# First loads reordered, warm-up without a load, and one weight split moved ahead of the first gates

## The chip, the cores and the metric

The kernel runs on one core of one Trainium2 chip. The metric is the device time of one execution in microseconds (us). Three runs of the kernel before gave 2299.57, 2301.09 and 2301.11, the median being 2301.09.

## The reference

A first block and a second block, each of two layers, work on `x` of 256 tokens by 1024 channels in float32. Each layer has a feed-forward part, a mixer and a second feed-forward part. The change touches only the start of the first feed-forward part of all:

```python
h = rmsnorm(x, g_ffn1[l])                       # x * rsqrt(mean(x^2) + 1e-6) * g
x = x + 0.5 * ((silu(h @ w1) * (h @ w3)) @ w2)  # w1, w3: 1024 x 2816, w2: 2816 x 1024
```

The mixers (Fourier, short convolution and pooling in the first block; window attention and gated linear attention in the second) follow, and the result is 256 x 1024 float32.

## The kernel before

All weights, some 400 MB, are streamed once, so every matmul works on a weight that has just arrived. A weight unit is 128 partitions by 2048 float32 columns, 1 MB, loaded by the SP engine into one of three `raw` buffers (`RAW = 3`) as two DMAs of 512 KB with 4 KB per partition. To keep float32 accuracy each weight and each activation is split in two rounded halves: ScalarE copies `raw` into `whi` (`split` at L1129), VectorE subtracts to get `wlo` (`split` at L1581), and TensorE multiplies hi by hi, hi by lo and lo by hi. `whi` and `wlo` have four slots (`HL = 4`). The semaphores are `raw_in` (loaded), `hi_done` (ScalarE's half), `w_ready` (VectorE's half, which also lets SP load the raw buffer anew), and `w_used` (multiplied, which lets ScalarE write the slot anew). SP's load of unit u waits until unit u - 3 is split on VectorE; SP issues its loads strictly in order, each waiting in front of all that follow.

In a feed-forward part unit b (0 to 21) holds, for one block of 128 hidden channels, the columns of the gate and of the up matrix for all eight 128-row chunks of the 1024 inputs. `hidden_chunks` (L640 to L660) multiplies it: 32 matmuls in 16 pairs, one of 512 columns (L656) and one of 256 (L657), into one of three pairs of PSUM banks. ScalarE's `low_parts(b)` copies the low part out (L1196), VectorE's `summed` adds it (L1710) and frees the banks (`pair_free`), `gate_scaled` multiplies the gate by `rstd_row` (L1715), ScalarE's `gates` applies Silu (L1202), VectorE's `hidden` multiplies by the up part (L1720), and ScalarE's `hidden_hi` (L1207) and VectorE's `hidden_lo` (L1726) split the result. These steps and the splits stand in one hand-written order on each engine.

The norm is spread over the part: the matmuls take x times the gain only; 1/rms comes in by `rstd_row`. It needs `x` in the token layout: ScalarE squares it (L1160) after both 512 KB loads of `x` have landed (`x_in`, 32), takes the root, VectorE refines it and makes a diagonal matrix with the identity (`rstd_diag`, L1660 to L1665), and TensorE spreads it (`rstd_spread`, L706) between the second and third chunk of unit 3. ScalarE copies the result to `rstd_row` (L1231), and only then can the gates of units 0 and 1 be done; the gates of unit 2 and the splits of units 5 and later follow these.

For the very first part the activations come transposed from the host (`t_xt`), in four pieces of two chunks, 256 KB with 2 KB per partition. They are multiplied by the norm weight columns `vecs` on ScalarE (L1154) and split on VectorE (L1612). The first halves of units 0 and 1 come as pieces of their own too (`first_piece`, L428). The identity and `vecs` (128 x 144) are loaded from ScalarE's queue. TensorE waits for the identity and runs `WARM = 16` transposes whose result nobody uses (L1105), then `begin` (L665 to L682): unit 0 chunks 0 and 1, unit 0 chunks 2 and 3, unit 1 chunks 0 to 3, then the upper halves of units 0 and 1, each when its split and its activations are there.

Of the kernel before, what the change touches and what calls it, by code (L numbers as in the profile page):

```python
# [27 lines left out]
P = 128  # L28
# [5 lines left out]
FG = FF // 256  # L34
FC = FF // P
EPS = 1e-6
WARM = 16
PAIR = (0, 2, 1)
SPACER = 40
RAW = 3  # L40
# [23 lines left out]
V_FOLDED = V_FINAL + DC  # L64
V_GAIN = {"ffn0": 0, "mix": DC, "ffn1": 2 * DC}
V_CONV = V_OUT_NORM = 3 * DC
FIRST_PARTS = tuple(slice(2 * i, 2 * i + 2) for i in range(4))


HEADS, KV_HEADS, HEAD_DIM = 8, 2, 64  # L70
# [78 lines left out]
def rows_of(first, n):  # L149
    return slice(first, first + n)  # L150
# [21 lines left out]
def build(nc, a, known):  # L172
# [4 lines left out]
    def semaphore(name):  # L177
        return ctx.enter_context(nc.semaphore(name))
# [7 lines left out]
    with ctx:  # L186
# [153 lines left out]
        x_in = semaphore("x_in")  # L340
        ident_in = semaphore("ident_in")
        vecs_in = semaphore("vecs_in")
        xt_part_in = [semaphore(f"xt_part_in{i}") for i in range(4)]
        warm = semaphore("warm")
        first_m = semaphore("first_m")
        out_ready = semaphore("out_ready")
# [57 lines left out]
        def _(eng):  # L404
# [21 lines left out]
            def first_piece(u, first, cols, signal):  # L426

                eng.dma_start(raw[:, u, first:first + cols], a["t_gate_up_1a"][rows_of(u * P, P), first:first + cols]  # L428
                              ).then_inc(signal, 16)
# [87 lines left out]
            def xt_part(i):  # L517
                cols = FIRST_PARTS[i]
                eng.dma_start(xt_in[:, cols, :], a["t_xt"].rearrange("p (c t) -> p c t", c=DC)[:, cols, :]
                              ).then_inc(xt_part_in[i], 16)  # L520
# [3 lines left out]
            xt_part(1)  # L524
            first_piece(0, 512, 512, first_in[1])
            first_piece(1, 0, 1024, first_in[2])
            for u in range(2):
                xt_part(2 + u)
                for j in range(2):
                    first_piece(u, 1024 + 512 * j, 512, raw_in[u])  # L530
            for u in (2, 3):
                gate_up(a["t_gate_up_1a"], u, u)
            for m in range(MT):
                eng.dma_start(x[:, m, :], a["x"][0, m * P:(m + 1) * P, :]).then_inc(x_in, 16)
            for _ in e.layers(1):
                ffn_loads(0, a["t_gate_up_1a"], a["w2_a"])
                if e.layer() == 0:
                    eng.dma_start(cs[:, :, :], a["t_cs"].rearrange("(m p) n -> p m n", p=P)).then_inc(tables1_in, 16)
                    eng.dma_start(cc[:, :], a["t_cc"]).then_inc(tables1_in, 16)
                    eng.dma_start(poolm[:, :, :, :], a["t_pool"].rearrange("(m p) (g t) -> p m g t", p=P, g=4)  # L540
                                  ).then_inc(tables1_in, 16)
                mix1_loads(FFN_UNITS)
                ffn_loads(FFN_UNITS + MIX_UNITS[1], a["t_gate_up_1b"], a["w2_b"])
# [25 lines left out]
        def _(eng):  # L569
# [530 lines left out]
                assert u + 2 == u0 + MIX_UNITS[2]  # L1100

            eng.sem_inc(w_used, HL)
            eng.wait_ge(ident_in, 16)
            for _ in range(WARM):
                nc.tensor.transpose(psum[:, 5, 0:P], ident[:, :], ident[:, :])  # L1105
            for _ in e.layers(1):
                ffn_tensor(0, 0, "mix")
                mix1_tensor(FFN_UNITS)
# [8 lines left out]
        def _(eng):  # L1117
# [71 lines left out]
            def ffn_scalar(u0, f, next_stage):  # L1189
                stage = f"ffn{f}"  # L1190

                def low_parts(b):

                    multiplied(u0 + b)
                    first = 2 * PAIR[b % 3]
                    nc.scalar.activation(low[:, b % 2, :, :], psum[:, first:first + 2, T:2 * T], ACT.Copy).then_inc(  # L1196
                        low_done, 1)

                def gates(b):

                    eng.wait_ge(scaled_done, ffn_blocks(e, f, b))
                    nc.scalar.activation(gate[:, b % 2, :], gate[:, b % 2, :], ACT.Silu).then_inc(gate_done, 1)  # L1202

                def hidden_hi(b):

                    eng.wait_ge(hid_done, ffn_blocks(e, f, b))
                    nc.scalar.activation(ht_hi[:, b, :], hid[:, b % 2, :], ACT.Copy).then_inc(ht_hi_done, 1)  # L1207

                if stage == "ffn0" and (e.block, e.lay) == (2, 0):
                    eng.wait_ge(x_whole, wholes(e))  # L1210
                    final_squares(1, 0).then_inc(acted, e.mark(acted, ("ss", "final")))
                    eng.wait_ge(xgf_done, 2)
                    final_squares(1, 1).then_inc(acted, e.mark(acted, ("ss", "ffn0")))
                    x_hi(stage, 1)
                elif e.unit(u0) > 0:
                    x_hi(stage, 1)
                else:
                    split(2)
                    low_parts(0)
                    split(3)  # L1220
                    low_parts(1)
                    eng.wait_ge(x_in, 32)
                stage_start(stage, u0, [junk[:, m, :] for m in range(MT)])
                if e.unit(u0) > 0:
                    low_parts(0)
                    split(u0 + 4)
                    low_parts(1)
                else:
                    split(u0 + 4)
                eng.wait_ge(small, e.after(small, ("rstd", stage)))  # L1230
                nc.scalar.activation(rstd_row[:, :], psum[:, 6, 0:T], ACT.Copy).then_inc(  # L1231
                    acted, e.mark(acted, ("rstd", stage)))
                for b in range(2):
                    gates(b)
                split(u0 + 5)
                for b in range(2):
                    hidden_hi(b)
                for b in range(2, FC):
                    low_parts(b)
                    gates(b)  # L1240
                    hidden_hi(b)
                    split(u0 + b + 4)
                for s in range(2 * FG + 1, FFN_UNITS):
                    if s == 2 * FG + 6:
                        if next_stage == "ffn0":
                            eng.wait_ge(folded, 1)
                        if next_stage != "end":
                            x_hi(next_stage, 0)
                        if next_stage == "ffn0" and (e.block, e.lay) == (1, LAYERS - 1):
                            final_squares(0, 0)  # L1250
                            eng.wait_ge(xgf_done, 1)
                            final_squares(0, 1)
                    split(u0 + s + 3)
# [281 lines left out]
                split(u0 + 37)  # L1535
                split(u0 + 38)

            eng.dma_start(ident[:, :], a["t_ident"]).then_inc(ident_in, 16)
            eng.dma_start(vecs[:, 0:V_FOLDED], a["t_vecs"]).then_inc(vecs_in, 16)
            eng.wait_ge(warm, 1)  # L1540
            nc.scalar.activation(ms[:, :], rt[:, :], ACT.Copy)
            eng.wait_ge(vecs_in, 16)
            eng.wait_ge(xt_part_in[0], 16)
            first_hi_of(0, 0)
            eng.wait_ge(w_used, 2)
# [6 lines left out]
            eng.wait_ge(first_in[2], 16)  # L1552
            nc.scalar.activation(whi[:, 1, 0:1024], raw[:, 1, 0:1024], ACT.Copy).then_inc(first_hi, 1)
            for u in range(2):
                eng.wait_ge(xt_part_in[2 + u], 16)
                first_hi_of(1, u)
                split(u)
            for _ in e.layers(1):
# [11 lines left out]
        def _(eng):  # L1570
# [133 lines left out]
            def ffn_vector(u0, f, next_stage):  # L1704
# [30 lines left out]
                if e.unit(u0) == 0:  # L1735
                    split(u0 + 2)
                    first_summed(0)
                    split(u0 + 3)
                    first_summed(1)
                    norm(stage, rstd)  # L1740
                    rstd_diag(stage)
                else:
                    stage_start(stage, u0, 1)
                if e.unit(u0) == 0:
                    fold = vecs[:, V_FOLDED:V_FOLDED + DC]
                    nc.vector.tensor_tensor(fold, vecs[:, V_FINAL:V_FINAL + DC], vecs[:, V_BASE[2]:V_BASE[2] + DC],
                                            ALU.mult).then_inc(folded, 1)
# [7 lines left out]
                eng.wait_ge(acted, e.after(acted, ("rstd", stage)))  # L1755
                for b in range(2):
                    gate_scaled(b)
                for b in range(2):
                    hidden(b)
                for b in range(2):  # L1760
                    hidden_lo(b)
                for b in range(2, FC):
                    eng.wait_ge(low_done, ffn_blocks(e, f, b))
                    e.link(summed(gate, b, 0))
                    gate_scaled(b)
                    summed(up, b, 1).then_inc(pair_free, 1)
                    eng.wait_ge(pair_free, ffn_blocks(e, f, b))
                    hidden(b)
                    split(u0 + b + 3)
                    hidden_lo(b)  # L1770
                split(u0 + FC + 3)
                for s in range(2 * FG + 1, FFN_UNITS - 1):
# [414 lines left out]
                split(u0 + 37)  # L2187

            nc.vector.memset(rt[:, :], 1.0).then_inc(warm, 1)
            eng.sem_inc(w_ready, RAW)  # L2190
            eng.sem_inc(x_whole, 1)
            eng.wait_ge(ident_in, 16)
            eng.wait_ge(vecs_in, 16)
            eng.wait_ge(xt_part_in[0], 16)
            first_lo_of(0, 0)
            for k in range(2):
# [9 lines left out]
            nc.vector.tensor_tensor(wlo[:, 1, 0:1024], raw[:, 1, 0:1024], whi[:, 1, 0:1024], ALU.subtract).then_inc(  # L2206
                first_ready, 1)
            for u in range(2):
                eng.wait_ge(xt_part_in[2 + u], 16)
                first_lo_of(1, u)  # L2210
                split(u)
            for _ in e.layers(1):
# [80 lines left out]
```

## Time and profile before

| what | us |
|---|---|
| median of three runs | 2301.09 |
| profiled execution, its own time | 2298.62 |
| its span, first to last instruction | 2296.8 |
| TensorE busy | 2277.3 |
| VectorE busy | 1537.3 |
| ScalarE busy | 1242.2 |

The page lists TensorE (PE) with 11,756 matmuls at 99% of the span. DVE is VectorE, ACT is ScalarE, SP the engine that issues most DMAs, PEld the weight loads of TensorE. A time in a row of the timeline is the start, in us from the first instruction, followed by the duration; what stands in brackets is the idle time of that engine just before, and what ended it. The mean granted clock of TensorE over the span is 0.998 of full speed.

### The profile page before, as it was taken

To read this page: it belongs to the slowest core of one execution; us is meant where nothing else is said; L and a number is where in the kernel's file an instruction comes from. 1 tells how busy PE (TensorE), PEld (TensorE's weight loads), DVE (VectorE), ACT (ScalarE), POOL (GpSimd) and SP (SyncE) were. 2 spreads that over 40 slices of the span, in tenths; PEclk is the share of its full clock that TensorE was granted. 3 is DMA by queue.
4 is the path that set the end of the run, shared out by engine and by line. 5 is a ranking of instruction groups with operands and counts; after the bars stand their busy time and mean duration, and the time that the engine had idled before them with its cause. 6 is when DMAs were issued, how large, how long until landed. Compare 5 with 4: busy or idle time off the path is not lost.

```text
span 2296.8 us, 29070 instructions
## 1 busy us (share of the span) xinstructions
PE 2277.3 (99%) x11756; PEld 1932.9 (84%) x11756; DVE 1537.3 (67%) x2156; ACT 1242.2 (54%) x1484; POOL 0.2 (0%) x4
## 2 busy tenths in 40 slices
PE   8999999999999999999999999999999999999999
PEld 7887888888888788888888888788888888878887
DVE  6764566765774466775776587667657747866773
ACT  6544445554653544654654585455456547645652
POOL 0000000000000000000000000000000000000000
PEclk9999999999999999999999999999999999999999
DMA  7556455555555445555555543545545545345553
GB/s 253 200 196 217 152 178 184 188 206 174 184 192 193 160 166 196 183 196 185 194 187 194 195 161 106 193 160 195 200 175 188 202 163 184 107 150 187 198 183 129
DMA packets 175802, 416.52 MB, mean 181 GB/s; under 512 B 16658, under 2 KB 21394, under 8 KB 175668
## 3 DMA queue, kind: packets, MB, share of 16 engines
q1 hardware_dynamic: 175380, 414.52, 52.2%
q8 instruction: 93, 1.52, 0.3%
q14 instruction: 41, 0.34, 0.0%
q10 hardware_dynamic: 288, 0.14, 0.0%
HBM read 413.55 MB, written 1.05 MB: 181 GB/s over the span
## 4 chain that ended last, share of the span: by engine, by line
PE 95%; DVE 2%; DMA 1%; ACT 1%; issue 0%; SPq 0%; ACTq 0%; DVEq 0%
PE psum L656 27%; PE psum L592 16%; PE psum L594 16%; PE psum L593 16%; PE psum L657 14%; PE psum L624 2%; DVE split_w L1581 1%; PE psum L928 1%; PE psum L756 1%; DMA raw<-t_gate_up_1a_dram 0%; PE psum L906 0%; PE psum L773 0%; DMA x<-x_dram 0%; ACT split_w L1129 0%; PE psum L897 0%
## 5 line engine op out<-in xcount | busy, mean ns | idle before, releaser
L1581 DVE TENSOR_TENSOR split_w<-raw,split_w 128x2048 fp32r<-128x2048 f32 (+2 forms) x408 | 886.2, 2178 | 308.4 <-ACT split_w L1129 307.3
L656 PE MATMUL psum<-xt,split_w 128*128 128x512 f32 x2816 | 982.7, 394 | 2.2 <-DVE split_w L1581 1.7
L1129 ACT ACTIVATE split_w<-raw 128x2048 fp32r<-128x2048 f32 (+2 forms) x408 | 740.8, 1824 | 331.5 <-PE psum L594 295.4
L657 PE MATMUL psum<-xt,split_w 128*128 128x256 f32 x2816 | 785.1, 279 | 0.0
L656 PEld LDWEIGHTS psum<-xt,split_w 128*128 128x128 f32 x2816 | 527.8, 187 | 124.5 <-DVE split_w L1581 2.1
L657 PEld LDWEIGHTS psum<-xt,split_w 128*128 128x128 f32 x2816 | 530.9, 189 | 0.3
L592 PE MATMUL psum<-split_w,xt 128*128 128x512 f32 (+1 forms) x736 | 292.8, 398 | 6.3 <-DVE split_w L1581 6.3
L594 PE MATMUL psum<-split_w,xt 128*128 128x512 f32 (+1 forms) x736 | 284.8, 387 | 0.0
L593 PE MATMUL psum<-split_w,xt 128*128 128x512 f32 (+1 forms) x736 | 284.8, 387 | 0.0
L592 PE MATMUL psum<-split_w,ht_hi 128*128 128x512 f32 x700 | 273.0, 390 | 0.0
L594 PE MATMUL psum<-split_w,ht_lo 128*128 128x512 f32 x700 | 272.5, 389 | 0.0
L593 PE MATMUL psum<-split_w,ht_hi 128*128 128x512 f32 x700 | 272.4, 389 | 0.0
L1710 DVE TENSOR_TENSOR gate<-psum,low 128x256 f32<-128x256 f32 x176 | 74.6, 424 | 155.4 <-ACT low L1196 155.2
L592 PEld LDWEIGHTS psum<-split_w,xt 128*128 128x128 f32 x736 | 139.0, 189 | 37.9 <-DVE split_w L1581 6.2
L594 PEld LDWEIGHTS psum<-split_w,xt 128*128 128x128 f32 x736 | 138.9, 189 | 28.5
L593 PEld LDWEIGHTS psum<-split_w,xt 128*128 128x128 f32 x736 | 139.2, 189 | 26.6 <-issue 1.0
L1196 ACT ACTIVATE low<-psum 128x512 f32<-128x512 f32 x176 | 104.6, 594 | 103.0 <-PE psum L657 102.7
L1202 ACT ACTIVATE gate<-gate 128x256 f32<-128x256 f32 x176 | 73.0, 418 | 161.3 <-DVE gate L1715 161.3
L594 PEld LDWEIGHTS psum<-split_w,ht_lo 128*128 128x128 f32 x700 | 131.4, 188 | 27.5
L592 PEld LDWEIGHTS psum<-split_w,ht_hi 128*128 128x128 f32 x700 | 131.4, 188 | 27.1
L593 PEld LDWEIGHTS psum<-split_w,ht_hi 128*128 128x128 f32 x700 | 131.4, 188 | 26.8
L1207 ACT ACTIVATE ht_hi<-hid 128x256 fp32r<-128x256 f32 x176 | 72.5, 416 | 90.4 <-DVE hid L1720 90.4
(272 smaller groups left out, 1730.8 us busy)
## 6 DMA issues: line engine op xcount, KB each, us to landing
raw<-w_in_dram SPq DMA_DIRECT2D x180, 512.0 KB, 4.4
raw<-t_gate_up_1b_dram SPq DMA_DIRECT2D x88, 512.0 KB, 4.1
raw<-t_gate_up_2a_dram SPq DMA_DIRECT2D x88, 512.0 KB, 4.1
raw<-t_gate_up_2b_dram SPq DMA_DIRECT2D x88, 512.0 KB, 4.1
raw<-t_gate_up_1a_dram SPq DMA_DIRECT2D x85, 512.0 KB, 4.1
raw<-ffn_w_down_dram SPq DMA_DIRECT2D x80, 512.0 KB, 4.3
raw<-w_a_dram SPq DMA_DIRECT2D x40, 512.0 KB, 4.1
raw<-w_b_dram SPq DMA_DIRECT2D x40, 512.0 KB, 4.2
```

Source lines behind the costliest of these rows:

```text
L592: nc.tensor.matmul(pair(p, m)[:, out], hi[:, c, t], whi[:, slot, w], start=first, stop=False)
L593: nc.tensor.matmul(pair(p, m)[:, out], hi[:, c, t], wlo[:, slot, w], start=False, stop=False)
L594: last = nc.tensor.matmul(pair(p, m)[:, out], lo[:, c, t], whi[:, slot, w], start=False, stop=final)
L624: last = nc.tensor.transpose(bank[0:src.shape[1], i * T + m * P:i * T + (m + 1) * P], src, ident[:, :])
L656: nc.tensor.matmul(bank, whi[:, slot, w], xt[:, c, :, :], start=c == 0, stop=False)
L657: last = nc.tensor.matmul(bank[:, 0:T], wlo[:, slot, w], xt_hi[:, c, :], start=False, stop=c == DC - 1)
L1129: nc.scalar.activation(whi[:, u % HL, first:n], raw[:, r, first:n], ACT.Copy).then_inc(hi_done, 1)
L1196: nc.scalar.activation(low[:, b % 2, :, :], psum[:, first:first + 2, T:2 * T], ACT.Copy).then_inc(low_done, 1)
L1202: nc.scalar.activation(gate[:, b % 2, :], gate[:, b % 2, :], ACT.Silu).then_inc(gate_done, 1)
L1207: nc.scalar.activation(ht_hi[:, b, :], hid[:, b % 2, :], ACT.Copy).then_inc(ht_hi_done, 1)
L1581: nc.vector.tensor_tensor(wlo[:, u % HL, first:n], raw[:, r, first:n], whi[:, u % HL, first:n], ALU.subtract).then_inc(w_ready, 1)
L1710: return nc.vector.tensor_tensor(out[:, b % 2, :], bank[:, 0:T], low[:, b % 2, j, :], ALU.add)
```

## The change

The edits, in the order of the diff:

- The activations come in three pieces: chunks 0-1, 2-3, and 4-7 (512 KB, 4 KB per partition). The last one is issued ahead of the upper halves of units 0 and 1, which come as two DMAs of 64 partitions with 4 KB per partition in place of two of 128 partitions with 2 KB.
- ScalarE's queue issues only the eight columns of `vecs` that the first norm needs, under a semaphore of its own (`gains_in`). The identity goes to SP's queue, behind unit 3 and ahead of `x`; the remaining 136 columns of `vecs` follow behind `x`.
- TensorE's warm-up is 11 float32 matmuls of 128 columns on zeros that VectorE writes to `junk`, in place of 16 transposes of the identity. It waits for that memset.
- VectorE waits for the identity at `rstd_diag` and for `vecs` at the fold behind it; ScalarE waits for `vecs` ahead of the first gates.
- In the first feed-forward part ScalarE does `low_parts(2)` and the split of unit 5 ahead of the first two gates, where the split stood behind them; VectorE does its split of unit 5 behind the two products with `rstd_row` and ahead of `hidden(0)`, where it stood behind `hidden(2)`. All other parts keep their order.

```diff
-WARM = 16
+WARM = 11
-FIRST_PARTS = tuple(slice(2 * i, 2 * i + 2) for i in range(4))
+FIRST_PARTS = (slice(0, 2), slice(2, 4), slice(4, 8))
...
             first_piece(1, 0, 1024, first_in[2])
+            xt_part(2)
             for u in range(2):
-                xt_part(2 + u)
-                for j in range(2):
-                    first_piece(u, 1024 + 512 * j, 512, raw_in[u])
+                for j in range(2):
+                    part = slice(64 * j, 64 * j + 64)
+                    eng.dma_start(raw[part, u, 1024:2048], a["t_gate_up_1a"][rows_of(u * P + 64 * j, 64), 1024:2048]
+                                  ).then_inc(raw_in[u], 16)
             for u in (2, 3):
                 gate_up(a["t_gate_up_1a"], u, u)
+            eng.dma_start(ident[:, :], a["t_ident"]).then_inc(ident_in, 16)
             for m in range(MT):
                 eng.dma_start(x[:, m, :], a["x"][0, m * P:(m + 1) * P, :]).then_inc(x_in, 16)
+            eng.dma_start(vecs[:, DC:V_FOLDED], a["t_vecs"][:, DC:V_FOLDED]).then_inc(vecs_in, 16)
...
-            eng.wait_ge(ident_in, 16)
+            eng.wait_ge(warm, 2)
             for _ in range(WARM):
-                nc.tensor.transpose(psum[:, 5, 0:P], ident[:, :], ident[:, :])
+                nc.tensor.matmul(psum[:, 5, 0:P], junk[:, 0, 0:P], junk[:, 0, 0:P], start=True, stop=True)
...
+                if e.unit(u0) == 0:
+                    eng.wait_ge(pair_free, ffn_blocks(e, f, 0))
+                    low_parts(2)
+                    split(u0 + 5)
+                    eng.wait_ge(vecs_in, 16)
                 for b in range(2):
                     gates(b)
-                split(u0 + 5)
+                if e.unit(u0) > 0:
+                    split(u0 + 5)
                 for b in range(2):
                     hidden_hi(b)
                 for b in range(2, FC):
-                    low_parts(b)
+                    if e.unit(u0) > 0 or b > 2:
+                        low_parts(b)
...
-            eng.dma_start(ident[:, :], a["t_ident"]).then_inc(ident_in, 16)
-            eng.dma_start(vecs[:, 0:V_FOLDED], a["t_vecs"]).then_inc(vecs_in, 16)
+            eng.dma_start(vecs[:, 0:DC], a["t_vecs"][:, 0:DC]).then_inc(gains_in, 16)
             eng.wait_ge(warm, 1)
             nc.scalar.activation(ms[:, :], rt[:, :], ACT.Copy)
-            eng.wait_ge(vecs_in, 16)
+            eng.wait_ge(gains_in, 16)
...
                     norm(stage, rstd)
+                    eng.wait_ge(ident_in, 16)
                     rstd_diag(stage)
                 else:
                     stage_start(stage, u0, 1)
                 if e.unit(u0) == 0:
+                    eng.wait_ge(vecs_in, 16)
                     fold = vecs[:, V_FOLDED:V_FOLDED + DC]
...
                 for b in range(2):
                     gate_scaled(b)
+                if e.unit(u0) == 0:
+                    split(u0 + 5)
...
-                    split(u0 + b + 3)
+                    if e.unit(u0) > 0 or b > 2:
+                        split(u0 + b + 3)
...
             nc.vector.memset(rt[:, :], 1.0).then_inc(warm, 1)
+            nc.vector.memset(junk[:, 0, 0:P], 0.0).then_inc(warm, 1)
...
-            eng.wait_ge(ident_in, 16)
-            eng.wait_ge(vecs_in, 16)
+            eng.wait_ge(gains_in, 16)
```

## Rows read from the trace of the kernel before

**Rows 1.** The page: the span, and busy time of each engine.

```profile
span 2296.8 us, 29070 instructions
PE 2277.3 (99%) x11756; PEld 1932.9 (84%) x11756; DVE 1537.3 (67%) x2156; ACT 1242.2 (54%) x1484; POOL 0.2 (0%) x4
```

**Rows 2.** Waits of PE, whole span: us in total, times, longest.

```profile
PE psum L592 <- DVE split_w L1581: 9.3, 6, 2.7
...
PE psum L656 <- DVE split_w L1581: 1.7, 2, 1.2
```

**Rows 3.** Timeline of the head: start us, us, engine, line.

```profile
0.73 0.41 ACTq L1538 DMA_DIRECT2D ident<-t_ident_dram  x1
...
4.05 3.67 PE L1105 MATMUL psum<-ident 128*128 128x128 f32 x16 [4.05 <-DMA ident<-t_ident_dram]
...
5.47 0.91 ACT L1154 ACTIVATE xt<-xt_in,vecs 128x256 fp32r<-128x256 f32 x2 [2.32 <-DMA vecs<-t_vecs_dram]
...
8.05 0.80 PE L656 MATMUL psum<-xt,split_w 128*128 128x512 f32 x1 [0.32 <-DVE split_w L2199]
```

**Rows 4.** DMA issues at 0.73, 1.16 and 4.54: KB, us to landing.

```profile
xt_in<-t_xt_dram SPq DMA_DIRECT2D x1, 256.0 KB, 3.1
vecs<-t_vecs_dram ACTq DMA_DIRECT2D x1, 72.0 KB, 4.3
...
raw<-t_gate_up_1a_dram SPq DMA_DIRECT2D x1, 256.0 KB, 7.7
```

**Rows 5.** Instructions on the tile `ones`: min/median/max ns.

```profile
L1661 DVE MEMSET ones<- x1: 165/165/165, 27.6 to 27.6; 128x128 f32 x1
```

**Rows 6.** Timeline of PE at 1380 us, float32 matmuls.

```profile
1380.25 1.05 PE L928 MATMUL psum<-sm 128*128 128x128 f32 x8
```

**Rows 7.** One-us stretches: busy by engine, then PE clock, DMA share, GB/s.

```profile
7.00:8.00 1.00, 0.72 (x4) 0.32 (x2) 1.00 (x3) 1.00 (x3) 0.00 (x0) 1.00 0.97 244
...
12.00:13.00 1.00, 1.00 (x7) 0.87 (x7) 0.83 (x2) 0.72 (x1) 0.00 (x0) 1.00 1.02 395
```

**Rows 8.** Chain that ended last, 12 to 23 us: start us, us.

```profile
13.37 1.24 DVE split_w L1581
14.62 0.33 SPq L415
...
15.95 6.86 DMA x<-x_dram
```

**Rows 9.** Timeline, 28 to 46 us.

```profile
28.24 0.70 PE L706 MATMUL psum<-diag,ones 128*128 128x256 f32 x2
...
29.76 1.28 ACT L1202 ACT_TABLE_LOAD   x1
31.71 0.75 DVE L1715 TENSOR_TENSOR gate<-gate,rstd_row 128x256 f32<-128x256 f32 x2
32.17 0.75 ACT L1202 ACTIVATE gate<-gate 128x256 f32<-128x256 f32 x2 [1.12 <-DVE gate L1715]
...
32.83 1.90 ACT L1129 ACTIVATE split_w<-raw 128x2048 fp32r<-128x2048 f32 x1
35.06 0.76 DVE L1726 TENSOR_TENSOR ht_lo<-hid,ht_hi 128x256 fp32r<-128x256 f32 x2 [1.68 <-ACT ht_hi L1207]
35.24 0.58 ACT L1196 ACTIVATE low<-psum 128x512 f32<-128x512 f32 x1
...
37.64 2.28 DVE L1581 TENSOR_TENSOR split_w<-raw,split_w 128x2048 fp32r<-128x2048 f32 x1
...
40.06 0.47 PE L656 MATMUL psum<-xt,split_w 128*128 128x512 f32 x1 [1.24 <-DVE split_w L1581]
...
42.27 2.28 DVE L1581 TENSOR_TENSOR split_w<-raw,split_w 128x2048 fp32r<-128x2048 f32 x1
...
45.69 0.39 PE L656 MATMUL psum<-xt,split_w 128*128 128x512 f32 x1
```

**Rows 10.** A slice of two us late in the span, columns as in rows 7.

```profile
1460.00:1462.00 2.00, 2.00 (x7) 1.57 (x6) 1.50 (x1) 0.00 (x0) 0.00 (x0) 0.54 0.76 260
```

More of the change, by code:

```diff
@@ L342, in build @@
         vecs_in = semaphore("vecs_in")
-        xt_part_in = [semaphore(f"xt_part_in{i}") for i in range(4)]
+        gains_in = semaphore("gains_in")
+        xt_part_in = [semaphore(f"xt_part_in{i}") for i in range(3)]
         warm = semaphore("warm")
@@ L1554, in _ @@
             for u in range(2):
-                eng.wait_ge(xt_part_in[2 + u], 16)
+                eng.wait_ge(xt_part_in[2], 16)
                 first_hi_of(1, u)
@@ L2208, in _ @@
             for u in range(2):
-                eng.wait_ge(xt_part_in[2 + u], 16)
+                eng.wait_ge(xt_part_in[2], 16)
                 first_lo_of(1, u)
```

## Prediction

> **What bounds the kernel now.** I read the page first: TensorE is busy for 99% of the span, so the kernel is a queue of matmuls and only an interval in which TensorE stands still, or runs slowly, can be won [rows 1]. The span is 2296.8 us and the profiled execution took 2298.62 us, that is 1.8 us around the span; the median of the runs shown is 2301.09, so 2.5 us above it. I make the sum as a difference on the profiled execution and set it against the median.
>
> The second view is what TensorE waited for. Matmuls of the mixers wait 9.3 us for VectorE, six times; a look at stretches of the span puts these behind 1250 us, in code that the change doesn't touch. In the first stage there are two waits for the split of weights (L1581), 1.7 us together [rows 2]. The timeline of the head shows the rest. TensorE does nothing until 4.05, when the identity has landed and the warm-up transposes can run; its first real matmul starts at 8.05. ScalarE starts on the activations at 5.47, released by the norm weights (`vecs`), and 2.58 us pass from there to 8.05 (two activation halves, a 512-column split on ScalarE, the same on VectorE) [rows 3]. The first real matmul pairs are slow (the first matmul took 0.80 us where later ones of the same shape take about 0.40).
>
> **Part 1, the first loads.** The norm weights are issued second on ScalarE's queue and land 4.3 us after their issue; the first activation piece, issued at 0.73 like the identity, lands after 3.1 us, so at 3.8 [rows 3, 4]. In the new kernel eight columns go first on that queue. I bound their landing from both sides by the 3.1 us and the 4.3 us of these two rows: 3.8 to 5.0, and take 3.8, the nearer in size. A weight piece of 256 KB follows and then lands near 5.0 (it was issued 0.45 us behind the activations and 136 KB of small rows are gone), which ScalarE reaches just then. So the first real matmul can start at 3.8 + 2.58 = 6.4, at most 7.6: 0.5 to 1.65 us earlier.
>
> A rule of the Trainium skill speaks against the eight columns: "DMA: Bandwidth & Descriptors", Specifications, says that transfers under 512 B are not at line rate because the engine reads, modifies and writes. The rows here are 32 B. It gives no time for so few of them; no row of this trace has 32 B either, and the bound of 5.0 us above doesn't use it.
>
> **The warm-up.** It no longer waits for the identity but for two memsets on VectorE; one of 128x128 takes 0.17 us [rows 5] and starts near 0.9, so TensorE starts at about 1.1. A float32 matmul is recorded as two passes; eight passes of 128x128 take 1.05 us at the full clock with the drain of the last [rows 6], 0.11 us each. The 16 transposes took 3.67 us in the cold state, 0.23 each [rows 3]. Eleven matmuls are 22 passes, 22 x 0.23 = 5.1 us, so they end at 6.2, just ahead of 6.4. If the passes did not overlap with their weight loads (0.42 each), the warm-up would end at 1.1 + 9.2 = 10.3. TensorE would then be busy for more than 5 us before the first real pair, where it was busy for 3.7 before: the slow first pairs, some 0.6 us over two pairs, should mostly be gone.
>
> **What follows in the head.** Each later piece is limited by its landing. Without the 136 KB, at about 290 GB/s at the head, all pieces come some 0.45 us earlier, those of the second stage too; then the upper activations come as one 512 KB piece ahead of the upper half of unit 0, where 256 KB stood before, which costs 256 KB at the 393 GB/s to be had there = 0.65 us. The upper half of unit 0 landed at 4.54 + 7.7 = 12.25 [rows 4, 7]. Rows of 4 KB instead of 2 KB work for it: the stretch with 2 KB and smaller rows moved 244 GB/s, the one at 12 us 395 [rows 7]; for the 768 KB changed that is between nothing and 768 KB x (1/0.244 - 1/0.395) = 1.2 us. I take 0.25, near the lower end, because 2 KB rows were also in flight at 395. The upper half of unit 0 lands at 12.25 - 0.45 + 0.65 - 0.25 = 12.2, between 11.3 and 12.5.
>
> This landing matters more than the first one. VectorE's split of unit 0 (ended at 14.6) frees the raw buffer for unit 3, whose load SP issues at 14.62, and behind it in the same queue stands `x`, which landed at 15.95 + 6.86 = 22.83 [rows 8]. Everything in the norm hangs on that landing. The identity now stands ahead of `x`: 64 KB, 0.17 us at 393 GB/s, 0.25 with its small rows. The shift of `x`'s landing is d = -0.05 + 0.2 = about +0.1, and by the bounds -0.7 to +0.5. The rest of `vecs` stands behind `x` and is asked for only at ScalarE's first gate and VectorE's fold, several us later. Unit 4's load, behind it, is 0.2 us later and had landed before 26, two us before its split.
>
> **Part 2, the sixth unit.** TensorE stopped at 38.82 and went on at 40.06, for VectorE's split of unit 5 (37.64, 2.28 us) [rows 9]. Now ScalarE, at 29.76 (where it loaded its table), first does `low_parts(2)` (0.58, pitch 0.50), then the split (1.90), to 32.16; the table load (1.28) and the two gates (0.75) follow to 34.1. VectorE has ended its two products with `rstd_row` at 31.71 + 0.75 = 32.46, then splits unit 5 to 34.7. So TensorE finds unit 5 ready 5 us early, and the 1.24 us go.
>
> What is late next: VectorE's `hidden(0)` comes behind that split, at 34.66; ScalarE's rounding at 35.07; VectorE's `ht_lo` at 35.5 where it was at 35.06. From here everything is 0.43 us later: `gates(2)`, `hidden(2)`, ScalarE's split of unit 6, then `low_parts(3)`, which was behind ScalarE's split of unit 6 before as well, and behind all that VectorE's split of unit 6, which was 42.27 to 44.55 [rows 9]. It now ends at 44.98 + d. TensorE began unit 6 at 45.69 (after unit 5 from 40.06), and would without a wait begin it at 45.69 - 1.24 = 44.45. So a wait of 0.6 us takes the place of the one of 1.24. Unit 7 follows 4.63 us behind unit 6 on VectorE (42.27 - 37.64) against 5.63 us of matmuls (45.69 - 40.06), so no later wait comes.
>
> Is the earlier head worth more? No: TensorE, if it comes to unit 3 earlier, waits at the spread of `rstd` (28.24 before, [rows 9]), which hangs on `x` by d. All that is won before it ends there. The sum: new start of unit 6 = 45.05 + d = 45.15, against 45.69: 0.55 us less. With 0.1 for small things I forecast 0.6 us less: 2298.0 on the profiled execution, 2300.5 on the median.
>
> The table load is where a rule and the trace differ. Before, the load at 29.76 stood behind a finished copy and cost 1.28 [rows 9]. The Trainium skill, "ScalarE: Activation LUTs", What ACT_TABLE_LOAD costs, adds a drain of about 1.38 us to each switch; by that the gates would end at 35.5 and the chain to unit 6 would be some 0.8 us later. The trace has nothing of that drain, and I go by 1.28.
>
> **The rivals.** (a) *The loads are faster than I count.* If 4 KB rows and the missing small rows bring `x` forward by 0.7 us (d = -0.7), unit 6 is ready at 44.35, the spread and all of TensorE's work behind it move too, and unit 6 begins at 44.35: 1.3 us less; with the bound of 1.2 us for the rows in full 1.9 less. That is 2299.8 to 2299.2. For it: 244 against 395 GB/s. Against it: that low rate belongs to the very first rows too, when queues fill.
>
> (b) *The upper activations in one piece delay everything.* The place is the landing of the upper half of unit 0, ahead of which 256 KB more now stand; the price goes one to one through the raw buffer of unit 3 to `x`, the norm and unit 6, with the identity's 0.25 on top. It decides from d = +0.64 (45.69 - 45.05). With nothing for rows and with columns of 32 B and 64-partition pieces each held up by some tenths, d is 0.5 to 1.2: slower by up to 0.6, 2301.5.
>
> (c) *The warm-up fails its purpose*: it ends at 10.3, or zeros leave the clock low. Then TensorE's first 32 pairs (5.63 / 16 = 0.352 us each, 11.3 us) end at 21.6, unit 2 at 27.2, and the spread, four pairs on, comes at 28.6, 0.4 late; without a wait unit 6 would start at 44.45 + 0.4 = 44.85, before it is ready. It is hidden, and the time is mine, 2300.5; clock staying low for 5 us longer would cost up to 2.5 us, 2302.
>
> (d) *The change doesn't do what it says*: TensorE still waits at unit 5 or an engine waits long for `vecs` or the identity: no change, 2301.1.
>
> **How the numbers follow.** My case 0.5, (a) 0.2, (b) 0.17, (c) with a loss and (d) 0.13 together. The measured medians also move: late in the span TensorE's granted clock fell to 0.54 in a slice of 2 us [rows 10], that is to its lower level of 1.2 GHz for most of it, after it had stood waiting for VectorE. That slice alone lost 2 x 0.46 = 0.9 us, it went on into the next, and it happened twice in this execution; I estimate 1.5 us for each, and suppose that their number differs between executions: the profiled one and the median differ by 2.5 us. So the range is 2297.8 to 2302.0. What a measurement can tell from no change is about 0.2%, 4.6 us; every case above lies inside it. Only something unseen gets out: 0.03 faster, 0.04 slower, 0.93 the same.
>
> **What would show it.** In the new profile: first warm-up matmul near 1.1, first real one at 6.2 to 7.6, the first pairs at 0.35 us; `x` landed at 22.1 to 23.3; no wait at unit 5 and a wait of 0.3 to 0.8 at unit 6; a small wait at the spread. I am wrong if TensorE reaches unit 7 more than 1.5 us earlier or any later than before, or if a wait for `vecs` shows up on ScalarE or VectorE.

## Result, and the profile after

The changed kernel took 2303.15 us (median of 20 runs, 2300.76 to 2305.33); the kernel before, run beside it, 2299.36 (20 runs, 2295.70 to 2301.93). The ratio is 1.0017, with a 95% interval of 1.0011 to 1.0024: 3.8 us slower, less than 0.2%, but clear of the noise. The forecast of 2300.5 us and its direction were wrong, and the time lies outside the range. The forecast started from 2301.09, the median of three runs; twenty runs put the kernel before at 2299.36, so as a difference the miss is larger: 0.6 us less was forecast, 3.8 us more was measured.

The page after, which answers to [rows 1]:

```profile
span 2302.6 us, 29085 instructions
PE 2279.3 (99%) x11762; PEld 1936.9 (84%) x11762; DVE 1537.9 (67%) x2157; ACT 1242.1 (54%) x1484; POOL 0.2 (0%) x4
```

The waits of TensorE over the span after (us in total, times, longest), for [rows 2]:

```profile
PE psum L597 <- DVE split_w L1592: 9.6, 6, 2.9
PE psum L661 <- DVE split_w L2215: 3.0, 2, 2.2
PE psum L661 <- DVE split_w L1592: 2.8, 3, 1.6
PE psum L661 <- DVE split_w L2222: 1.9, 1, 1.9
PE psum L1110 <- DVE junk L2206: 1.1, 1, 1.1
PE psum L711 <- DVE diag L1675: 0.9, 1, 0.9
```

The mixers' waits are as before (9.6 for 9.3). New are waits for each of the first splits. The timeline of the head (start us, us; in brackets the idle time and what ended it) says what they waited for. It answers to [rows 3]:

```profile
0.73 0.41 ACTq L1550 DMA_DIRECT2D vecs<-t_vecs_dram  x1
...
1.08 4.97 PE L1110 MATMUL psum<-junk 128*128 128x128 f32 x22 [1.08 <-DVE junk L2206]
...
4.24 0.91 ACT L1159 ACTIVATE xt<-xt_in,vecs 128x256 fp32r<-128x256 f32 x2 [1.58 <-DMA vecs<-t_vecs_dram]
...
6.82 0.50 PE L661 MATMUL psum<-xt,split_w 128*128 128x512 f32 x1 [0.77 <-DVE split_w L2215]
...
9.29 0.63 ACT L1562 ACTIVATE split_w<-raw 128x512 fp32r<-128x512 f32 x1 [1.62 <-DMA raw<-t_gate_up_1a_dram]
...
11.96 1.06 ACT L1564 ACTIVATE split_w<-raw 128x1024 fp32r<-128x1024 f32 x1 [2.04 <-DMA raw<-t_gate_up_1a_dram]
...
14.51 0.91 ACT L1159 ACTIVATE xt<-xt_in,vecs 128x256 fp32r<-128x256 f32 x2 [1.49 <-DMA xt_in<-t_xt_dram]
...
16.66 1.06 ACT L1134 ACTIVATE split_w<-raw 128x1024 fp32r<-128x1024 f32 x1 [1.24 <-DMA raw<-t_gate_up_1a_dram]
...
27.98 1.06 ACT L1165 ACTIVATE junk<-x 128x1024 f32<-128x1024 f32 x1 [0.95 <-DMA x<-x_dram]
```

TensorE starts its warm-up at 1.08 and its real work at 6.82, 1.2 us earlier than before, as forecast. Then the pieces fall behind: the upper half of unit 0, which landed at 12.25 before, comes at 16.66, and `x` at 27.98 instead of 22.83. What the DMA engines did meanwhile (slices of one us: all engines' busy time, then PE clock, DMA share, GB/s; [rows 7] are the slices at 7 and 12 us before):

```profile
7.00:8.00 1.00, 1.00 (x7) 0.86 (x8) 0.22 (x1) 0.68 (x2) 0.00 (x0) 1.00 1.09 340
...
12.00:13.00 1.00, 0.38 (x3) 0.05 (x1) 0.00 (x0) 1.00 (x1) 0.00 (x0) 1.00 1.01 238
...
15.00:16.00 1.00, 1.00 (x7) 0.89 (x6) 0.48 (x2) 0.41 (x2) 0.00 (x0) 1.00 1.04 176
```

The engines are as busy as before (share 1.0) and move half: 176 to 238 GB/s where before it was 395. They don't wait for work; each packet takes longer. Grouping the trace's packets by size and time says the same: a packet of 4 KB took 159 ns on average from 13 to 15 us before, and, slice by slice, about 270 to 390 ns from 10 to 16 us after.

The chain of waits (answers to [rows 8]) and the end of the head (answers to [rows 9]):

```profile
4.12 12.51 DMA raw<-t_gate_up_1a_dram
16.66 1.07 ACT split_w L1134
17.75 1.24 DVE split_w L1592
19.00 0.33 SPq L416
...
20.80 7.16 DMA x<-x_dram
```

```profile
33.39 0.70 PE L711 MATMUL psum<-diag,ones 128*128 128x256 f32 x2 [0.85 <-DVE diag L1675]
...
37.36 1.28 ACT L1207 ACT_TABLE_LOAD   x1 [0.17 <-DVE gate L1726]
38.65 0.73 ACT L1207 ACTIVATE gate<-gate 128x256 f32<-128x256 f32 x2
...
47.73 2.28 DVE L1592 TENSOR_TENSOR split_w<-raw,split_w 128x2048 fp32r<-128x2048 f32 x1
...
50.16 0.47 PE L661 MATMUL psum<-xt,split_w 128*128 128x512 f32 x1 [0.81 <-DVE split_w L1592]
```

Unit 6 starts at 50.16 where it was 45.69, 4.5 us later; from there on the two kernels do the same. The profiled executions differ by 5.75 us (2304.37 and 2298.62). The rest, 1.3 us, is about what the granted clock late in the span accounts for: it stood at 0.50 over three slices of 2 us, a loss of 3.0 us, where the kernel before had 0.54 for one ([rows 10]) and 0.61 for the next, a loss of 1.7 (an estimate, 2 us times what is missing to 1.00 in each slice):

```profile
1464.00:1466.00 2.00, 1.95 (x5) 1.56 (x6) 2.00 (x1) 0.00 (x0) 0.00 (x0) 0.50 0.43 103
1466.00:1468.00 2.00, 2.00 (x6) 1.58 (x5) 0.20 (x1) 0.00 (x0) 0.00 (x0) 0.50 1.04 394
1468.00:1470.00 2.00, 2.00 (x8) 1.54 (x7) 0.00 (x0) 0.00 (x0) 0.00 (x0) 0.50 0.91 327
```

### The profile page after: what moved, and what is told of

Read it like the earlier page. It is cut to its first block, busy times and chain, and to the rows that moved or that the text cites. A ratio compares the mean times of both kernels' runs of the same rounds, so it can differ in the third digit from the quotient of the medians.

```text
span 2302.6 us, 29085 instructions
## 1 busy us (share of the span) xinstructions
PE 2279.3 (99%) x11762; PEld 1936.9 (84%) x11762; DVE 1537.9 (67%) x2157; ACT 1242.1 (54%) x1484; POOL 0.2 (0%) x4
## 4 chain that ended last, share of the span: by engine, by line
PE 96%; DVE 2%; DMA 1%; ACT 1%; issue 0%; SPq 0%; ACTq 0%; DVEq 0%
PE psum L661 27%; PE psum L597 16%; PE psum L599 16%; PE psum L598 16%; PE psum L662 14%; PE psum L629 2%; DVE split_w L1592 1%; PE psum L933 1%; PE psum L761 1%; DMA raw<-t_gate_up_1a_dram 1%; DMA x<-x_dram 0%; PE psum L911 0%; PE psum L778 0%; PE psum L902 0%; ACT split_w L1134 0%
```

## Experiments

Since run times of one kernel scatter by some 6 us, I read each experiment first by where unit 6 starts in its profile, then by its median. "Upper half" is the landing of unit 0's upper half (ScalarE's split starts there), "squares" is where ScalarE begins the squares of `x`. The ratio is that of the run times, this kernel over the one before. Each profile is one execution: with the same first loads as before, the upper half came between 11.45 and 12.28 in five profiles, and the squares began between 22.62 and 23.56 in the three of them that also load `x` as before and have no other change to the loads. Differences below about 0.9 us between two rows are therefore not told from scatter.

| kernel | upper half | squares | unit 6 | median, us (before beside it) | ratio, 95% |
|---|---|---|---|---|---|
| before | 12.28 | 22.83 | 45.69 | 2299.36 | |
| changed | 16.66 | 27.98 | 50.16 | 2303.15 (2299.36) | 1.0011 to 1.0024 |
| changed, second look | 16.21 | 28.08 | 50.26 | 2305.45, one run (2298.12) | |
| 128 partitions, 2 KB | 12.56 | 24.20 | 46.38 | 2300.16 (2299.32) | 0.9998 to 1.0016 |
| 128 partitions, 4 KB | 12.81 | 24.83 | 46.94 | 2300.57 (2299.32) | 0.9995 to 1.0012 |
| 64 rows, even and odd | 12.75 | 23.32 | 45.50 | 2300.01 (2298.94) | 0.9999 to 1.0017 |
| before, 64 partitions only | 14.14 | 25.21 | 48.08 | 2301.01 (2299.32) | 0.9999 to 1.0017 |
| before, sixth unit only | 11.67 | 22.62 | 44.80 | 2297.76 (2299.32) | 0.9988 to 1.0006 |
| before, warm-up only | 12.00 | 23.56 | 46.43 | 2299.36 (2298.94) | 0.9990 to 1.0009 |
| four pieces | 12.08 | 23.89 | 46.07 | 2298.47 (2298.94) | 0.9989 to 1.0007 |
| small loads early | 11.85 | 23.40 | 45.59 | 2297.65 (2298.94) | 0.9988 to 1.0006 |
| x early | 11.85 | 19.04 | 44.59 | 2297.26 (2298.12) | 0.9988 to 1.0006 |
| x early, old head | 12.17 | 19.31 | 44.98 | 2298.49 (2298.12) | 0.9989 to 1.0006 |

Where unit 6 has no wait or unit 5 has it, 5.63 us were added to the start of unit 5 (40.80 with the warm-up only, 42.45 with 64 partitions only), or the pair nearest to the end of the split was taken (46.94, 128 partitions with 4 KB). The run with unit 2 alone over 64 partitions stands in its own section.

### 128 partitions with 2 KB, and with 4 KB

The changed kernel with the upper halves of units 0 and 1 loaded over all partitions: as two pieces of 512 columns,

```diff
-                    part = slice(64 * j, 64 * j + 64)
-                    eng.dma_start(raw[part, u, 1024:2048], ...[rows_of(u * P + 64 * j, 64), 1024:2048])...
+                    first_piece(u, 1024 + 512 * j, 512, raw_in[u])
```

> The changed kernel, but the upper halves of units 0 and 1 come as in the kernel before: two pieces of 128 partitions with 2 KB each. Theory H (pieces of 64 partitions slow down every transfer in flight): the upper half of unit 0 lands near 12.5 us, x near 23, 4 KB packets never average over 250 ns in the head, unit 6 starts at 45.0 to 45.7; 0.3 to 0.8 us below the kernel before. Rival O (512 KB of activations ahead of the weights): landing stays near 16 us and the time 3 to 4 us above the kernel before. Rival G (the 32 B rows of eight columns hold up the queues): the same 3 to 4 us above.

or as one piece of 1024 columns.

```diff
+                eng.sem_inc(raw_in[u], 16)
+                first_piece(u, 1024, 1024, raw_in[u])
```

> The changed kernel, but each upper half comes as one piece of 128 partitions with 4 KB. H: like the kernel with 2 KB rows or up to 0.5 us better (landing 12.0 to 12.5, unit 6 at 44.6 to 45.6), so 0.3 to 1.2 us below the kernel before. If instead 4 KB rows in the head are what is slow: 3 to 4 us above it. O and G: 3 to 4 us above.

In both the landing returns to 12.6 and 12.8, and unit 6 to 46.4 and 46.9: 3.8 and 3.2 us of the 4.5 are gone. The slow loads come with the pieces of 64 partitions, as H has it; O and G, as causes of the whole, are ruled out. I had expected both to be ahead of the kernel before, and neither is: `x` comes at 24.2 and 24.8, not 23. And rows of 4 KB are not faster than rows of 2 KB: from 12 to 14 us the two versions moved 420 (2 KB) and 410 GB/s (4 KB). The run times point the same way but say less: the medians are 0.8 and 1.3 us above the kernel before where the changed kernel is 3.8 above it, and the intervals of their ratios, up to 1.0016 and 1.0012, overlap with that of the changed kernel.

### The kernel before with 64 partitions only

```diff
-                    first_piece(u, 1024 + 512 * j, 512, raw_in[u])
+                    part = slice(64 * j, 64 * j + 64)
+                    eng.dma_start(raw[part, u, 1024:2048], ...[rows_of(u * P + 64 * j, 64), 1024:2048])...
```

> The kernel before with one part of the change alone: upper halves of units 0 and 1 as two pieces of 64 partitions with 4 KB. H: the upper half of unit 0 lands 3 to 4.5 us later than 12.25, x 3 to 5 us later than 22.8, and the time is 3 to 5 us above the kernel before. O and G: within 0.5 us of it.

The upper half of unit 0 comes 1.9 us later, the squares 2.4, unit 6 2.4. From 10 to 16 us this kernel moved 228 to 252 GB/s with a DMA share of 1.0, where the kernel before moved 391 to 414 up to 14 us. The direction is H's, the size is below what I expected: alone, among the four activation pieces, the same loads cost 2.4 us, and in the changed kernel, where four of them stand in a row behind 512 KB of activations, 3.2 to 4.7. Why the order makes that difference wasn't isolated.

### 64 rows over even and odd partitions

The changed kernel, its pieces still of 64 rows of 4 KB, but over every second partition:

```diff
-                    eng.dma_start(raw[part, u, 1024:2048], ...[rows_of(u * P + 64 * j, 64), 1024:2048])...
+                    eng.dma_start(raw[j:P:2, u, 1024:2048], ...[u * P + j:u * P + P:2, 1024:2048])...
```

> The changed kernel with its pieces of 64 rows of 4 KB laid over even and over odd partitions instead of the lower and upper 64. Theory P (64 neighbouring partitions are reached by only part of the ways into SBUF): full rate returns, the upper half of unit 0 lands at 12.5 to 13.0, 4 KB packets take 160 to 210 ns on average from 10 to 16 us, unit 6 at 46.3 to 47. Theory N (pieces of 64 rows are slow wherever they go): landing near 16.6 and unit 6 near 50, as in the changed kernel.

This tells the number of rows from their place. The same number of packets of the same size, issued in the same order, lands at 12.75, and unit 6 starts at 45.50, 4.7 us ahead of the changed kernel and 0.8 ahead of what I expected. First the slices of 2 us of the changed kernel, then of this one (slice, POOL busy, PE clock, DMA share, GB/s):

```profile
10.00:12.00 2.00, 0.00 (x0) 1.00 1.02 195
12.00:14.00 2.00, 0.00 (x0) 1.00 1.03 236
14.00:16.00 2.00, 0.00 (x0) 1.00 1.04 213
```

```profile
10.00:12.00 2.00, 0.00 (x0) 0.78 1.03 416
12.00:14.00 2.00, 0.00 (x0) 0.50 1.01 412
```

With the DMA engines equally busy, 64 neighbouring partitions take 195 to 236 GB/s and 64 spread ones 412 to 416; a packet of 4 KB took 159 ns there from 10 to 16 us. Theory P holds against N: it is which 64 partitions, not how many rows. The Trainium skill, "SBUF — State Buffer", Door 1: The DMA port swizzle, has the mechanism: bit 6 of the partition number chooses one of a cluster's two ports, so partitions 0 to 63 reach 8 of 16 ports; it gives 196 GB/s for 1 MiB. These runs agree with the rate; the ports themselves they don't show. One rival is not closed by this edit: the even and odd pieces read every second row of the weights in HBM too, so their source changed with their target. The traces speak against it, though they don't close it. Each load of `x` is 512 KB from one stretch of HBM, spread over 128 partitions, and while these were in flight the kernel before moved 410 and 414 GB/s (20 to 22 us). The pieces of the next experiment are 512 KB from one stretch too, and they were slow.

### Unit 2 alone over 64 partitions

```diff
-            for u in (2, 3):
-                gate_up(a["t_gate_up_1a"], u, u)
+            for j in range(2):
+                eng.dma_start(raw[64 * j:64 * j + 64, 2, :], ...[rows_of(2 * P + 64 * j, 64), :]).then_inc(raw_in[2], 16)
+            gate_up(a["t_gate_up_1a"], 3, 3)
```

> The kernel before with unit 2 alone loaded as two pieces of 64 neighbouring partitions with 8 KB each, in place of two of 128 with 4 KB. If 64 partitions have half the rate: 1 MB takes 2.5 to 2.8 us longer than at about 390 GB/s, unit 2 lands at 19 to 19.5 where it was 16.8, and the GB/s fall to about 200 from 14 to 18 us. If pieces of 64 partitions do no harm: 16.5 to 17.

The disputed cost by itself, in the kernel before and with twice the bytes; the rows are 8 KB here where they were 4 KB, which this run doesn't tell apart. Slices as above, and ScalarE's splits of unit 1 and unit 2:

```profile
12.00:14.00 2.00, 0.00 (x0) 1.00 1.10 169
14.00:16.00 2.00, 0.00 (x0) 1.00 1.05 211
16.00:18.00 2.00, 0.00 (x0) 1.00 0.96 190
18.00:20.00 2.00, 0.00 (x0) 1.00 1.03 156
```

```profile
15.85 1.06 ACT L1131 ACTIVATE split_w<-raw 128x1024 fp32r<-128x1024 f32 x1 [2.54 <-DMA raw<-t_gate_up_1a_dram]
...
21.49 1.91 ACT L1131 ACTIVATE split_w<-raw 128x2048 fp32r<-128x2048 f32 x1 [4.58 <-DMA raw<-t_gate_up_1a_dram]
```

Unit 2 lands 4.7 us later than at 16.77, more than I expected, and the upper half of unit 1, issued before it and over all partitions, is at least 1.6 us late as well (it had landed by 14.27 before). So such a piece costs more than its own bytes at half the rate: what is in flight around it slows down too. The one run took 2303.34 us, 5.2 above the median of the kernel before.

### The changed kernel again

> The changed kernel once more, to see how far its head repeats. If the slow landing is part of the kernel: upper half of unit 0 at 16 to 17, x at 27 to 28.5, unit 6 at 49.5 to 50.5. If it was chance of one execution: below 15, 25 and 48.

No edit. Landing 16.21, squares 28.08, unit 6 at 50.26: within 0.5 us of the first look. The slow landing is part of the kernel and not of one execution.

### Sixth unit only, warm-up only

The kernel before with the edits of ScalarE's and VectorE's order alone, as in the change, and another with the warm-up on zeros alone.

> The kernel before with the other part alone: low part of unit 2 and split of unit 5 ahead of the first gates. As predicted: the wait of 1.24 us at unit 5 goes, a wait of 0.6 us at unit 6 comes, unit 6 starts at 45.05 instead of 45.69; 0.6 us less. If the order itself costs (gates late): unit 6 at 46 or later and no gain.

> The kernel before with the warm-up on zeros alone. The first pairs of real matmuls run at 0.35 us a pair, not 0.6, but unit 5 waits for the same split: unit 6 at 45.7 and the time within 0.5 us of the kernel before. If the early matmuls disturb the first loads: the second piece of unit 0 lands 1 us later than near 7.6.

The sixth unit does what was worked out. Its wait has moved to unit 6, TensorE first, for the split of VectorE:

```profile
44.80 0.47 PE L656 MATMUL psum<-xt,split_w 128*128 128x512 f32 x1 [0.82 <-DVE split_w L1587]
```

Unit 6 starts 0.9 us earlier, of which 0.2 come from an earlier landing of `x`. In the time this can't be told from no change. The warm-up alone brings the first real pair forward by 0.3 us and, with `x` 0.7 us later in that execution, nothing at unit 6. Pairs at 0.35 us, which I expected from the start, it did not have: the second pair took 0.54 us, and pairs of 0.64 followed, as the granted clock fell (last section).

### Four pieces, and small loads early

From the kernel with 128 partitions and 2 KB: the activations again in four pieces in the old order; and then also the identity and the rest of `vecs` between the loads of units 2 and 3.

```diff
             gate_up(a["t_gate_up_1a"], 2, 2)
+            eng.dma_start(ident[:, :], a["t_ident"]).then_inc(ident_in, 16)
+            eng.dma_start(vecs[:, DC:V_FOLDED], ...).then_inc(vecs_in, 16)
             gate_up(a["t_gate_up_1a"], 3, 3)
...
```

The lines of these two loads at their old places, behind unit 3 and behind `x`, are left out here.

> The changed kernel with upper halves as two pieces of 128 partitions and 2 KB, and also the activations in four pieces of 256 KB in the order of before. Left of the change: eight columns first, identity ahead of x, vecs behind it, warm-up on zeros, sixth unit. Rival O (512 KB of activations ahead): second piece of unit 0 lands near 7.3 instead of 8.6, upper half of unit 0 by 12.0, x by 23.6, unit 6 at 45.7. If the order does not matter, only the small loads do: x at 24.0 to 24.4 and unit 6 at 46.2 to 46.6, as with 128 partitions alone.

> As the kernel with four pieces, with the identity and the rest of vecs issued between the loads of units 2 and 3, where the DMA engines run partly idle, so that nothing small stands around x. Theory S (the small loads ahead of and behind x delay its landing by 1 us and more): x lands 1.0 to 1.5 us earlier than with them around x, at 22.6 to 23.0, unit 6 at 44.6 to 45.2, 0.6 to 1.1 us below the kernel before. If the small loads cost only their bytes: x 0.2 us earlier.

Both expectations hold in part. With four pieces the second piece of unit 0 is split at 7.78 instead of 8.64, and the upper half lands 0.5 us earlier; the price of 512 KB ahead, forecast as 0.65, is about right. The first pair took 0.80 us and the next four 0.64 each in that profile, after a warm-up of the usual length, and not 0.35: the warm-up doesn't do its work in every execution. Moving the small loads away brings `x` forward by 0.5 us only, where theory S expected at least 1. Between ScalarE's split of unit 3 and the squares lie 3.7, 4.0, 4.2, 3.4, 2.9 and 3.9 us in the six profiles with the identity ahead of `x`, and 2.8, 2.7, 3.4 and 2.9 in four with the small loads elsewhere (the two versions of the kernel before with 64 partitions are left out, since ScalarE hardly waited for `x` there): 0.7 us on average, with ranges that overlap. I leave its size open.

### x early

The order that the runs point to: `x` ahead of unit 3's load, ScalarE's squares ahead of its split of unit 3, VectorE's norm ahead of the sums of unit 1. Once on the kernel with small loads early, once on the kernel before with the sixth unit.

ScalarE's part of the edit:

```diff
+                    eng.wait_ge(x_in, 32)
+                    squares(stage, [junk[:, m, :] for m in range(MT)])
                     split(3)
                     low_parts(1)
-                    eng.wait_ge(x_in, 32)
...
+                    root(stage)
...
```

> The version that the runs point to: eight columns first, four activation pieces and upper halves with 128 partitions, warm-up on zeros, sixth unit early; and x is loaded ahead of unit 3 (identity and vecs behind it), where the queues run half idle, with the squares ahead of ScalarE's split of unit 3 and VectorE's norm ahead of the sums of unit 1. If x's landing is what sets the end of the head: x lands at 17 to 19, no wait at the spread, unit 6 starts at 43.4 to 44.4, 1.3 to 2.3 us below the kernel before. Rival: unit 3 comes too late behind x (split ready after 27) and TensorE waits there: unit 6 at 45 or later.

> The kernel before, with the sixth unit early and x ahead of unit 3 in the same way, but its own first loads and its warm-up with the identity. If the first loads of the change are worth something once x is out of the way: unit 6 about 0.5 to 1 us later than in the version with them (44.3 to 45.0). If not: the same.

The last two waits in the head of the first one, TensorE alone:

```profile
20.73 0.51 PE L659 MATMUL psum<-xt,split_w 128*128 128x512 f32 x1 [0.26 <-DVE split_w L1594]
...
44.59 0.47 PE L659 MATMUL psum<-xt,split_w 128*128 128x512 f32 x1 [0.52 <-DVE split_w L1594]
```

The squares start at 19.04, the wait at the spread is gone, and unit 6 starts at 44.59, 1.1 us ahead of the kernel before, less than the 1.3 to 2.3 expected: unit 3 now lands at 22.0 and takes `x`'s place at the root of the chain. The old head does nearly as well (44.98): the first loads and the warm-up are worth some 0.4 us, by one execution of each, which is within the scatter. The first of the two has the earliest unit 6 of all and the lowest median, 2297.26 us; it beats the changed kernel, but against the kernel before the interval of its ratio (0.9988 to 1.0006) still holds no change. The sixth unit alone (44.80) gets most of it.

## Why the prediction was wrong

**The first loads, up to the first real matmul: right.** Eight columns landed 3.5 us after their issue (3.1 to 4.3 forecast), TensorE was warming from 1.08 (1.1) for 4.97 us (5.1), the first real matmul came at 6.82 (6.4 to 7.6), and the first pairs took 0.35 us.

**What follows in the head: the step that failed.** I wrote that rows of 4 KB "work for it", between nothing and 1.2 us, took 0.25, and had the upper half of unit 0 land at 12.2, "between 11.3 and 12.5". It landed at 16.66. The term that I gave the sign of a gain is a loss of about 4.1 us (16.66 less the 12.56 with 128 partitions): 4 KB rows came with pieces of 64 neighbouring partitions, and these halved the rate. The gain itself is nil: 12.81 with whole 4 KB pieces against 12.56 with 2 KB. The 244 GB/s at 7 us that I had read as the rate of 2 KB rows wasn't theirs: in the kernel before, undisturbed packets of 2 KB took 84 ns and of 4 KB 159, over 16 engines 390 and 412 GB/s. Nor did the 0.45 us for the missing small rows come: with the old order of pieces the upper half landed at 11.85 to 12.08 in three profiles without them and at 11.45 to 12.28 in five with them. The 0.65 for 256 KB more ahead holds, with 0.8 between the averages of those three and of the three at 12.56 to 12.81.

I named the pieces only in rival (b), at "some tenths", and bounded the rate from rows in which every transfer spanned 128 partitions. No row of the kernel before shows a transfer over part of the partitions; the bound on its cost should have come from there, open on the slow side.

**From the landing to x: right in its mechanism, small in size.** The landing was 4.4 us late, and 4.4 went into unit 3's load, which SP issued at 19.00 instead of 14.62; the identity's slot on SP added 0.5 and the flight of `x` 0.3, and the norm and unit 6 followed, as rival (b) has it. It decides from d = 0.64, and d was 5.15: by my own sum 45.05 + 5.15 = 50.20, and unit 6 started at 50.16. So rival (b) had the path right and its price, up to 1.2, too small by far. With 128 partitions `x` still comes 1.4 and 2.0 us later than before (0.5 in the even and odd version), where I had 0.1 and a bound of 0.5; up to 0.9 of such a difference can be scatter. The issue slot of the identity (0.48 us) was missing from my sum, and 0.25 for its bytes may be too little; what makes up the rest stays open.

**The sixth unit: right.** Unit 6 was to start at 22.83 + 22.22 + d. In seven profiles with the new order it started 22.18 or 22.19 us after the squares began (27.98 to 50.16, 28.08 to 50.26, 22.62 to 44.80, 23.32 to 45.50, 23.40 to 45.59, 23.89 to 46.07, 24.20 to 46.38), and the wait there was 0.5 to 0.8. The head start of TensorE ended at the spread, as said: 0.85 us of waiting there, and 1.8 in the whole 4 KB version.

**The table load: the trace was the better guide.** In the changed kernel too the load is done after 1.28 us and the gates follow at once (37.36 to 38.65), with no drain behind it.

## What to carry to other kernels

Split a transfer along its columns, or over every second partition, and not into lower and upper 64 partitions; the change's pieces of 64 neighbours moved about 200 GB/s with all DMA engines busy, and cost 4 us in a head of 45. When a DMA share of 1.0 comes with few GB/s, look at where the bytes go, not at how many requests there are. And find the landing at the root of the chain first (here `x`, through a raw buffer that had to come free): gains ahead of it that don't move it are worth nothing.

## What the runs showed that I had not expected

TensorE's granted clock fell within the head in three profiles. With the warm-up alone it fell after a pause from 5.6 to 7.8, between the zeros and the first real pair, and in the even and odd version after one from 8.1 to 10.2, behind the first four pairs, each of 2.2 us. In the second look at the changed kernel it stood at 0.50 from 20 to 23 us, after a pause of 1.8 us that ended at 18.58. With the warm-up alone:

```profile
9.00:10.00 1.00, 1.00 (x4) 0.50 0.89 309
10.00:11.00 1.00, 1.00 (x5) 0.50 1.03 391
```

The share of 0.50 is the lower level, 1.2 GHz. In its first look the changed kernel had pauses of 2.20, 1.95 and 1.65 us and kept its clock, so this differs between executions of one and the same kernel. It cost nothing at unit 6 here, since TensorE waited for unit 5 or 6 even so.

A transfer issued later can delay an earlier one: with the 512 KB of activations behind it, the second piece of unit 0 (issued at 2.12) was split at 8.64 to 9.29 in five profiles, and at 7.49 to 8.05 in three with 256 KB behind it and the same small loads in front. The rows of the 512 KB are 4 KB long, those of the 256 KB 2 KB, and I didn't test which of the two matters, the length or the bytes.
